# The p projection moved ahead of the gate products in a two-block transformer kernel

## The reference, cut to what matters

```python
for i in range(DEPTH_2):
    ...
    gate = jax.nn.sigmoid(rmsnorm(h, ple_norm_g[i]) @ ple_gate_w[i])   # 1024 x 1024
    h = h + gate * (p[i] @ ple_proj_w[i])                              # 256 x 1024
```

## Time and profile before

| what | value |
|---|---|
| median of three runs | 1906.88 us (1901.38 to 1907.42) |
| the profiled execution's own time | 1906.07 us |
| its span, first to last instruction | 1904.3 us |
| mean granted TensorE clock | 0.973 of full |
| TensorE busy with products | 95% of the span |
| VectorE busy, ScalarE busy | 73%, 64% |

### The profile page before, as it was taken

One profiled execution on the slowest core, in us unless ns is written; L12 is line 12 of the kernel. 1 busy time (PEld: TensorE's weight loads), 2 busy tenths in 40 slices (PEclk: granted clock), 3 DMA queues, 4 the chain that ended last, 5 costly groups with the idle time before them and its releaser, 6 DMA issues.

```text
span 1904.3 us, 26803 instructions
## 1 busy us (share of the span) xinstructions
PE 1812.1 (95%) x9562; PEld 1545.7 (81%) x9562; DVE 1394.7 (73%) x1653; ACT 1219.2 (64%) x1536; POOL 5.9 (0%) x13
## 2 busy tenths in 40 slices
PE   8999979989999989869999999999999999999997
PEld 7877768979998779768888878788788787887885
DVE  4466755755665466558989899898998998989984
ACT  5546545644443355537778777687877777878773
POOL 0000000000000000000000000000000000000000
PEclk9899989999999999969999999999999999999999
DMA  9752223425445344318989899899898998998980
GB/s 325 250 182 95 80 97 133 155 97 197 177 177 204 128 170 165 113 46 325 378 314 374 328 360 368 327 359 377 319 368 324 357 374 322 371 353 339 367 330 23
DMA packets 68336, 483.32 MB, mean 254 GB/s; under 512 B 7610, under 2 KB 7738, under 8 KB 10928
## 3 DMA queue, kind: packets, MB, share of 16 engines
q1 hardware_dynamic: 66480, 475.26, 65.6%
q0 software_dynamic: 1792, 7.18, 1.8%
HBM read 478.22 MB, written 4.19 MB: 253 GB/s over the span
## 4 chain that ended last, share of the span: by engine, by line
PE 75%; DVE 11%; issue 7%; ACT 7%; DMA 0%; DVEq 0%; ACTq 0%; POOLq 0%
PE ps L1483 18%; PE ps L1484 18%; PE ps L1488 18%; DVE wlo L904 6%; PE ps L1728 4%; PE ps L1735 4%; PE ps L1729 4%; ACT whi L561 3%; PE ps L1466 3%; PE ps L1940 1%; PE ps L1941 1%; ACT xgh L858 1%; DVE sg L1027 1%; ACT sg L684 1%; PE ps L1831 1%
## 5 line engine op out<-in xcount | busy, mean ns | idle before, releaser
L904 DVE TENSOR_TENSOR wlo<-raw,whi 128x1024 fp32r<-128x1024 f32 x906 | 1044.0, 1213 | 168.3 <-ACT whi L561 167.8
L561 ACT ACTIVATE whi<-raw 128x1024 fp32r<-128x1024 f32 x906 | 903.4, 1055 | 140.9 <-PE ps L1488 118.8
L1483 PE MATMUL ps<-whi,xgh 128*128 128x512 f32 x896 | 355.5, 397 | 4.6 <-ACT whi L561 4.6
L1484 PE MATMUL ps<-whi,xgl 128*128 128x512 f32 x896 | 349.9, 391 | 0.0
L1488 PE MATMUL ps<-wlo,xgh 128*128 128x512 f32 x896 | 277.5, 391 | 0.0
L1483 PE MATMUL ps<-whi,xh 128*128 128x512 f32 (+1 forms) x448 | 188.0, 420 | 21.1 <-issue 9.8
L1483 PEld LDWEIGHTS ps<-whi,xgh 128*128 128x128 f32 x896 | 169.0, 189 | 38.4 <-ACT whi L561 4.8
L1488 PEld LDWEIGHTS ps<-wlo,xgh 128*128 128x128 f32 x896 | 168.8, 188 | 35.8
L1484 PEld LDWEIGHTS ps<-whi,xgl 128*128 128x128 f32 x896 | 169.1, 189 | 33.3
L1484 PE MATMUL ps<-whi,xl 128*128 128x512 f32 (+1 forms) x448 | 182.7, 408 | 0.0
L1483 PE MATMUL ps<-whi,mTh 128*128 128x512 f32 x448 | 175.7, 392 | 0.0
(11 more groups left out here) (288 smaller groups left out, 1895.7 us busy)
## 6 DMA issues: line engine op xcount, KB each, us to landing
raw<-in_w_moe_dram SPq DMA_DIRECT2D x336, 1024.0 KB, 7.1
raw<-in_w_fixed_dram SPq DMA_DIRECT2D x112, 1024.0 KB, 4.9
bias_scratch<-revb POOLq DMA_DIRECT2D x1, 3072.0 KB, 38.3
bias<-bias_scratch POOLq DMA_DIRECT2D x1, 2048.0 KB, 16.8
raw<-in_w_fixed_dram SPq DMA_DIRECT2D x4, 512.0 KB, 4.2
tok<-in_xt_dram SPq DMA_DIRECT2D x2, 512.0 KB, 4.6
h<-in_x_dram SPq DMA_DIRECT2D x1, 1024.0 KB, 13.9
out_dram<-h SPq DMA_DIRECT2D x2, 512.0 KB, 2.7
```

Of the source, the lines that this page charges most:

```text
L561: AC(whi[:, v % SPL, c], raw[:, v % RAW, c], ACT.Copy).then_inc(high_done, 1)
L904: V.tensor_tensor(wlo[:, v % SPL, c], raw[:, v % RAW, c], whi[:, v % SPL, c].bitcast(F32), ALU.subtract).then_inc(low_done, 1)
L1483: mm(o, hi(k0 + k, T), wh[:, k, :], start=first and k == 0, stop=False)
L1484: mm(o, lo(k0 + k, T), wh[:, k, :], start=False, stop=False)
```

## The change

In both `ple` stages the two p blocks come first and the two gate blocks after them; the weight units are packed and the end units of the blocks listed in that sequence. The p products are evacuated by ScalarE to `pm` in SBUF, which now holds both halves; VectorE multiplies `pm` by `pg` in place after the Sigmoid. For i = 0, `turn_rows(3, 0)` leaves the last dense unit and stands between the two p blocks; for i = 1, `turn_rows(6, 0)` stands behind both. `ptTh` and `ptTl` move from the feed-forward region into the second half of `tok`'s space; for i = 0 they are made during the dense part, for i = 1 at the head of `ple(1)`. `root` writes its unused squares for k = 3 and 6 to `gt` and `ht`.

```diff
     def ple(i):
-        return (block(("ple_gate_w_2", i), 0) + block(("ple_gate_w_2", i), NB)
-                + block(("ple_proj_w_2", i), 0, kt=2) + block(("ple_proj_w_2", i), NB, kt=2))
+        return (block(("ple_proj_w_2", i), 0, kt=2) + block(("ple_proj_w_2", i), NB, kt=2)
+                + block(("ple_gate_w_2", i), 0) + block(("ple_gate_w_2", i), NB))
...
-    ple_end = [2, 4, 5, 6]
+    ple_end = [1, 2, 4, 6]
...
-        tok = sb("tok", [P, NT, D])
+        with ExitStack() as a:
+            tok = sb("tok", [P, NT, D], scope=a)
+        with ExitStack() as a:
+            sb("tok_front", [P, D], scope=a)
+            ptTh = sb("ptTh", [P, 2, S], F32R, scope=a)
+            ptTl = sb("ptTl", [P, 2, S], F32R, scope=a)
+        sb("tok_words", [P, NT * D])
...
-                pm = sb("pm", [P, NT, NB], scope=a)
+                pm = sb("pm", [P, 2, NT, NB], scope=a)
...
# ScalarE
+            def p_high(i):
+                act.wait_ge(p_loaded, 16 * (i + 1))
+                AC(ptTh[:], pt_in[:], ACT.Copy).then_inc(ph_done, 1)
...
+                    if f == 1:
+                        p_high(0)
...
             def ple(i):
                 ub, bb = U[f"ple{i}"], B[f"ple{i}"]
-                start(3 * i + 3, ub)
+                if i:
+                    p_high(i)
+                split_to(ub + 2)
+                evac(bb, pm[:, 0])
+                turned_high(3 * i + 3, 0)
+                split_to(ub + 3)
+                evac(bb + 1, pm[:, 1])
+                turned_high(3 * i + 3, 1)
+                root(3 * i + 3)
                 for j in range(2):
-                    split_to(min(ub + 2 * j + 1 + AHEAD, ub + 5))
-                    b = bb + j
-                    evac_scaled(b, 3 * i + 3, pg[:, j], func=ACT.Sigmoid)
-                    if j == 0:
-                        act.wait_ge(p_loaded, 16 * (i + 1))
-                        AC(ptTh[:], pt_in[:], ACT.Copy).then_inc(ph_done, 1)
-                split_to(ub + 5)
+                    split_to(ub + 5)
+                    evac_scaled(bb + 2 + j, 3 * i + 3, pg[:, j], func=ACT.Sigmoid)
...
# VectorE
+            def p_low(i):
+                dve.wait_ge(ph_done, i + 1)
+                V.tensor_tensor(ptTl[:], pt_in[:], ptTh[:].bitcast(F32), ALU.subtract).then_inc(pl_done, 1)
...
+                    if f == 2:
+                        p_low(0)
...
-                split_to(ub)
+                if i:
+                    p_low(i)
+                split_to(ub + 2)
                 turned_low(3 * i + 3, 0)
-                split_to(ub + 1)
+                split_to(ub + 3)
                 turned_low(3 * i + 3, 1)
-                split_to(ub + 2)
                 invert_root(3 * i + 3)
-                split_to(ub + 3)
-                dve.wait_ge(ph_done, i + 1)
-                V.tensor_tensor(ptTl[:], pt_in[:], ptTh[:].bitcast(F32), ALU.subtract).then_inc(pl_done, 1)
...
+                split_to(ub + 5)
                 for j in range(2):
                     b = bb + 2 + j
                     if i == 0 and j == 0:
                         split_to(ub + 6)
 
-                    dve.wait_ge(banks_free[(b - 2) % 2], g.freed(b - 2))
-                    dve.wait_ge(half_used, g.through(b))
-                    if i or j:
-                        dve.wait_ge(h_half, 2 * i + j)
-                    V.tensor_tensor(pm[:], ps[:, pair(b):pair(b) + 2, :], pg[:, j], ALU.mult)\
-                        .then_inc(banks_free[b % 2], 1)
                     dve.wait_ge(banks_free[b % 2], g.freed(b))
+                    step(V.tensor_tensor(pm[:, j], pm[:, j], pg[:, j], ALU.mult))
                     c = slice(j * NB, (j + 1) * NB)
-                    V.tensor_tensor(h[:, :, c], h[:, :, c], pm[:], ALU.add).then_inc(h_half, 1)
+                    V.tensor_tensor(h[:, :, c], h[:, :, c], pm[:, j], ALU.add).then_inc(h_half, 1)
...
# TensorE
             def ple(i):
                 ub, bb = U[f"ple{i}"], B[f"ple{i}"]
+                pe.wait_ge(pl_done, i + 1)
+                for j in range(2):
+                    block(ub + j, bb + j, tile_of(ptTh), tile_of(ptTl), kt=2)
+                    if j == 0 and i == 0:
+                        turn_rows(3, 0)
                 if i:
                     turn_rows(6, 0)
-                block(ub, bb, *X, norm=3 * i + 3)
-                block(ub + 2, bb + 1, *X)
-                pe.wait_ge(pl_done, i + 1)
-                for j in range(2):
-                    block(ub + 4 + j, bb + 2 + j, tile_of(ptTh), tile_of(ptTl), kt=2)
+                block(ub + 2, bb + 2, *X, norm=3 * i + 3)
+                block(ub + 4, bb + 3, *X)
```

More of the change, by code:

```diff
@@ L270, in build @@
             with ExitStack() as a:
-                ptTh = sb("ptTh", [P, 2, S], F32R, scope=a)
-                ptTl = sb("ptTl", [P, 2, S], F32R, scope=a)
                 pg = sb("pg", [P, 2, NT, NB], scope=a)
-                pm = sb("pm", [P, NT, NB], scope=a)
+                pm = sb("pm", [P, 2, NT, NB], scope=a)
         ps = ctx.enter_context(nc.psum_tensor("ps", [P, 8, NB], F32))
@@ L564, in root @@
             def root(k):
-                unused = sg[:].rearrange("p a r n -> p (a r n)").rearrange("p (t d) -> p t d", t=NT) if k == 0 else tok
+                if k == 0:
+                    unused = [sg[:, i].rearrange("p r n -> p (r n)") for i in range(NT)]
+                elif k in (3, 6):
+                    unused = [x[:].rearrange("p t n -> p (t n)") for x in (gt, ht)]
+                else:
+                    unused = [tok[:, i, :] for i in range(NT)]
                 for i in range(NT):
-                    ins = AC(unused[:, i, :], h[:, i, :], ACT.Square, accum_out=st[:, i:i + 1])
+                    ins = AC(unused[i], h[:, i, :], ACT.Square, accum_out=st[:, i:i + 1])
                 step(ins)
@@ L1752, in dense @@
                     for half in range(2):
-                        last = k0 == nk - KU and half == 1
                         products(u, KU, NB, tile_of(hTh), tile_of(hTl), k0,
-                                 [ps[:, 4 + 2 * T + half, :] for T in range(NT)], k0 == 0, k0 == nk - KU,
-                                 (lambda: turn_rows(3, 0)) if last else None)
+                                 [ps[:, 4 + 2 * T + half, :] for T in range(NT)], k0 == 0, k0 == nk - KU)
                         u += 1
```

1 line of the change is left out of this document (removed).

## The result

The change made the kernel slower: 1911.69 us at the median (1907.92 to 1915.83) against 1904.57 (1901.38 to 1907.42), a ratio of 1.0035 with a 95% interval of 1.0021 to 1.0049, or 4 to 9 us. The forecast time of 1910 was 1.7 us too low. The likeliest case was "same", with 0.3% or 1912.6 us as the line to slower: the ratio, 0.35%, lies beyond that line, and the time itself inside it, because the kernel before came out 2.3 us lower than the median on which the line was drawn. The forecast difference was 3.6 us and the measured one is 6.7. The profiled execution of before, on which the sum was made, lay 1.5 us above the median that more runs gave; that of after (1907.92, span 1906.1) is the fastest of its runs.

What follows compares the result with a forecast made beforehand. TensorE, busy for 95% of the span, bounds the kernel, so a change of order pays only in gaps. Layer 0's 1.6 us and layer 1's 2.0 make 3.6 on 1906.07: 1909.7, given as 1910; range 1904 to 1915.

Steps and rivals of the forecast that it cites:

- same: Whole kernel: measured time between 1901.2 and 1912.6 us, no difference that can be told; chance 0.65.
- the gate of layer 0 3.2 us later: Layer 0, gate start: first gate product at 659.55 instead of 656.33, behind p products, turn, evacuation, `xh` and `xl`.
- its chain from the second Sigmoid to h unchanged: Layer 0, stage end: the same 11.7 us to the next mixer, now with no products in them.
- the gate of layer 1 late by the p products: Layer 1, gate start: at 1873.1, 6.2 us late, as the turn stands behind both p blocks.
- its tail 4.2 us shorter: Layer 1, after the last gate product: 8.0 us become 3.85 of Sigmoid, `pm`, h and hand-overs.
- I take full clock ... so 1.6 back: Layer 0, first 12 gate products: 3.0 us in place of 4.57 behind a smaller gap; lower bound of gain nothing.
- so no clock is lost there that isn't now: Next mixer after layer 0: starts 1.6 us later, its first products already behind a 3.40 us gap; no added clock loss.
- the first rival, of falling clock: Layer 1, p products: clock falls after 2.8 us idle; 12 slow products give 1912.1, 24 give 1914.5; chance 0.25.
- The h update to the first p product: Layer 1, start of p products: h ends at 1862.23, `ptTl` takes 0.69 us, p products start at 1863.0.
- The base: Whole kernel: the profiled execution's 1906.07 us, to which 3.6 us were added; 0.8 under the median of the runs.
- The p products keep the clock up for the gate: Layer 1, first 12 gate products: 3.0 us in place of 4.88, whole kernel 1908; chance 0.12.
- The next mixer's turn starts with the second Sigmoid: Layer 0, behind the gate: chain of 6.7 us in place of 11.7, whole kernel 1905; chance 0.08.

Runs made afterwards that it cites:

- split_early: Changed kernel with ScalarE's split of the next mixer's first unit put ahead of layer 0's second Sigmoid: 1.0009 of the kernel before's time.
- l1_only: Kernel before with only layer 1 in the new order, layer 0 kept in the old one: 1.0018 of the kernel before's time.
- The fills: Changed kernel and kernel before, each with products nobody reads added in TensorE's idle stretches: 1.0009 and 0.9978 of the unfilled kernel before's time.
- fill_gaps: Changed kernel with products nobody reads added in three of TensorE's idle stretches: 1.0009 of the kernel before's time, twice the same.

## Why the prediction was partly right

**The order, right.** Every step of the order was as worked out: the gate of layer 0 3.2 us later, its chain from the second Sigmoid to h unchanged with no products in it, the gate of layer 1 late by the p products, its tail 4.2 us shorter. With the clock taken out, 5.2 us forecast stand against 5.5 in the traces and 5.9 in the ratios.

**The clock, wrong.** The gain of "I take full clock ... so 1.6 back" came: filling the gap of layer 0 in the kernel before gives the same 1.5 us (41.0 less 39.5). The step that failed in layer 0 is "so no clock is lost there that isn't now": 0.9 us went at the turn of the next mixer, which had the p products 1.8 us ahead of it and now stands behind 7.2 idle microseconds. I priced the first products of the mixer behind that gap and forgot the eight transposes in front of them. In layer 1 the first rival, of falling clock, was partly real: the first five p products or so ran at full clock, and some eight behind them 0.43 us apart, 1.6 us in all. They did so in both traces of the change and about so in `split_early`, and not in `l1_only`. On the other side the gate's own products took 0.9 us less than before, where I had left them the same, and the p products started 0.4 us later than forecast. In the traces the sum closes: 3.6 forecast, 0.9 for the turn, 1.6 and 0.4 for the p products, less 0.9 for the gate, is 5.6.

How much of the clock's cost the change makes over all executions is less sure. The fills take 5.0 us from the changed kernel and 4.2 from the one before, a net of 0.8 us lost, where the prediction had a net of 1.6 gained; but each of the two is good to about 3 us only, so that these ratios alone would not tell the one net from the other. That 0.9 is lost at the turn is shown by `fill_gaps` and by the five traces that have the slow turn; the share of layer 1 changes from execution to execution.

**Smaller terms.** The h update to the first p product took 1.1 us, not 0.8: 0.21 us before `ptTl` and 0.22 behind it. The base was high, by 1.5 us for the profiled execution and 2.3 for the median of three runs, and that hid part of the missing cost: that the time came so near the forecast 1910 is in part luck, since the forecast difference was little more than half of the measured one. A difference of 0.3% was also too coarse a line for what can be told: the interval of the whole change is 0.14% either way.

**The rivals.** "The p products keep the clock up for the gate" is open by execution: in the traces of the change most of the first 12 gate products of layer 1 run at half clock (a mean of 0.66 over 4.39 us), in `l1_only` all at full clock. The Trainium skill, page "TensorE: Matmul & The Clock Gate", section "What's actually happening", says that activity releases the throttle, and that the number of products at half clock differs from run to run of one kernel. The traces agree with the second statement: the gate's first 12 products of layer 1 take 4.23 us in one trace of the changed kernel and 4.34 in the other (in the same order 2.85 in `l1_only` and 5.28 in `split_early`). The fills agree with the first, by the granted clocks given there. "The next mixer's turn starts with the second Sigmoid" did not come, for the reason given, and `split_early` shows that an early turn was one line away and worth 5 us.

## What to carry to other kernels

Work moved into a gap leaves a gap where it was: before moving products, ask what they cover at their old place, and count what runs behind that place too, down to a handful of transposes. Here the p products were hidden behind a chain of 11.7 us at the end of a stage; moving them to the front paid clearly only when two waits were moved with them, the split of the next unit ahead of the last Sigmoid, and the turn ahead of the p products that can cover `xh` and `xl`. And put a transfer or a turn that others wait for at the first point at which its input is ready, not behind independent work of the same engine.

## What the hardware showed that I had not expected

Products that nobody reads, put into idle stretches of TensorE, made the kernel before 0.22% faster (interval 0.08 to 0.36) and the changed one 0.26% faster, with a mean granted clock of 0.978 and 0.979 in place of 0.973 and 0.975; eight transposes of 128x128 took 1.97 us at half clock against 1.09. And the same order of products ran its layer 1 in anything from 41.0 to 45.5 us by where the clock fell, 4.5 us, which is two thirds of the effect that was to be found.
